# Recurrent output projection: six of eight channel tiles as high and low parts, one unit's low parts by GpSimd

## The chip, the cores and the metric

The kernel runs on one NeuronCore of a Trainium2 chip. Its engines are TensorE (PE in the rows; its weight loads are PEld), VectorE (DVE), ScalarE (ACT), GpSimd (POOL) and SyncE (SP), which here only issues DMAs. They run side by side and wait for each other through semaphores. The metric is the time of one execution on the device in microseconds, lower being better; the median of several runs counts.

## What is computed

A decoder trunk of two layers on 256 tokens of width 1024, all in float32. Layer 0 is latent attention and a dense SwiGLU; layer 1 is a gated linear recurrence and a mixture of 8 experts, two for each token. The change sits at the end of the recurrence:

```python
    _, hs = lax.associative_scan(combine, (a, b), axis=1)
    y = hs.astype(h.dtype) * gate_br
    return y @ w_out            # (256 x 1024) @ (1024 x 1024)
...
    # in the trunk
    h = h + mix
    hn = rmsnorm(h, norm_ffn[i])
    h = h + moe_swiglu(hn, moe_w_router[k], moe_w_gate[k], moe_w_up[k], moe_w_down[k])
    return rmsnorm(h, norm_final)
```

## The kernel before

Everything is written out by hand: each engine has its own program, in a fixed order, with explicit waits on semaphores. Tokens are two tiles of 128 (`t`), output columns two halves of 512 (`b`), and the 1024 channels over which the projection sums are eight tiles of 128 (`a`). Weights arrive in units of 128 x 2048 float32 (1 MB), each holding two channel tiles of `w_out`, in the six slots of `raw`. The four units of `w_out` are `L_OUT` to `L_OUT + 3`, in slots 3, 4, 5 and 0.

The kernel multiplies in float32 in two ways.

- **Directly** (line 1473): float32 operands, with the stationary side cut into four strips of 32 tokens that work beside each other in the array. Each matmul of the program leaves two records in the trace.
- **As high and low parts** (`product`, lines 424 to 426): both operands are split into a rounded high part (type float32r) and the remainder. Three products, high by high, high by low and low by high, are added up in PSUM, each 128 x 128 by 128 x 512. The high part is a copy by ScalarE (`copy`, line 791; `split_hi`, line 398), the low part a subtraction of two SBUF tensors by another engine (`split_lo`, line 404, and line 2114).

In the projection before, channel tiles 0 to 3 (units `L_OUT`, `L_OUT + 1`) go directly, tiles 4 to 7 as parts. The direct part starts when the first half of y (`states[:, 0:4]`) has been multiplied by the gate (`gated(0)`, line 2086, `y_ready` 1). While TensorE works on it, VectorE does the second half of the recurrence: one multiplication (line 2074), four scans along the tokens (line 2076), `gated(1)` (line 2086, `y_ready` 2), then `out_low(0)` (line 2114), the low part of y tiles 4 to 7 (line 2119) and `out_low(1)`. ScalarE makes the high parts: of unit `L_OUT + 2` into `w_hi[:, 2]`, of `L_OUT + 3` into the memory of `xTl_lru`, and of y tiles 4 to 7 into `y_split`. TensorE waits for `y_lo` and for each unit's `lo_done`.

What follows the projection is a chain of small steps: the residual sum (line 2132), transposes of it (line 1431), the router's logits (line 1443), the choice of experts, and the gathering of each expert's tokens (line 1506). Then the experts' matmuls (line 1500) run to the end of the program. GpSimd is not used in the projection. Behind its wait for `y_ready` 2 it issues three small loads (lines 725 to 727, among them `wr`, the router's weights, that line 2124 needs) and makes constants for the router (lines 728 to 744). SyncE loads the experts' units in a ring of 16 places (lines 609 to 616), some of which are the slots of `raw`: slot 5 and slot 0 come free by `lo_done`, slots 3 and 4 by `used`, all four in the projection.

Of the kernel before, what the change touches and what calls it, by code (L numbers as in the profile page):

```python
# [6 lines left out]
F32 = mybir.dt.float32  # L7
# [14 lines left out]
def trunk(nc, x, positions, norm_mix, norm_ffn, norm_final, mla_w_in, mla_q_norm, mla_kv_norm,  # L22
# [25 lines left out]
    with ExitStack() as ctx:  # L48
# [5 lines left out]


        raw = sb(ctx, "raw", [P, SLOTS, UNIT], F32)
        res = sb(ctx, "res", [P, TT, D], F32)
# [18 lines left out]
        with ExitStack() as split:  # L76
# [18 lines left out]
            with ExitStack() as s:  # L95
# [8 lines left out]
                with ExitStack() as s2:  # L104
                    a_sq = sb(s2, "a_sq", [P, KT // 2, T], F32)
                xch = sb(s, "xch", [P, 2, T], F32R)
                xcl = sb(s, "xcl", [P, 2, T], F32R)
# [101 lines left out]
        def lru_use(n):  # L209
            return n % SLOTS, LRU_BASE + n // SLOTS + 1  # L210
# [423 lines left out]
        def _(pool):  # L634
# [87 lines left out]
            pool.memset(x_br[:, :, 0:CONV - 1], 0.0).then_inc(pads, 1)  # L722
            token_roots()
            pool.wait_ge(y_ready, 2)
            pool.dma_start(gain_moe[:], norm_ffn[1].partition_broadcast(P)).then_inc(moe_in, 16)
# [63 lines left out]
        def _(act):  # L789
# [250 lines left out]
            gate_out(6, ACT.Gelu_apprx_tanh)  # L1040
            gate_out(7, ACT.Gelu_apprx_tanh)
            for n, place in ((0, 2), (1, 1)):
                s, c = lru_use(L_OUT + 2 + n)
                act.wait_ge(landed[s], c * 16)
                act.wait_ge(used[place], SPLIT_USES[place])
                copy(OUT_SPLIT[n][0], raw[:, s]).then_inc(hi_done[s], 1)
# [72 lines left out]
        def _(pe):  # L1119
# [345 lines left out]
            for t in range(TT):  # L1465
                for b in range(2):
                    for a in range(4):
                        s, n = lru_use(L_OUT + a // 2)
                        if t == 0 and b == 0 and a % 2 == 0:
                            pe.wait_ge(landed[s], n * 16)  # L1470
                        for rows_q in QUARTERS:
# [3 lines left out]
                                           stop=False, tile_position=(0, rows_q.start), skip_group_check=True)  # L1475
                        if (t, b) == (TT - 1, 1) and a % 2 == 1:
                            mm.then_inc(used[s], 1)

            pe.wait_ge(y_lo, 1)
            for t in range(TT):  # L1480
                for b in range(2):
# [225 lines left out]
        def _(dve):  # L1707
# [403 lines left out]
            def out_low(n):  # L2111
# [3 lines left out]
                                  ALU.subtract).then_inc(lo_done[s], 1)  # L2115

            out_low(0)
            dve.wait_ge(y_hi, 1)
            dve.tensor_tensor(y_split[:, 1], states[:, 4:KT], y_split[:, 0].bitcast(F32),
# [301 lines left out]
```

## Time and profile before

| | before |
|---|---|
| median of 3 runs | 1317.88 us (1317.78 to 1318.00) |
| the profiled execution, its own time | 1318.05 us |
| its span, first to last instruction | 1316.2 us |
| TensorE busy in the span | 1305.8 us (99%) |
| direct part of the projection (64 matmuls, 128 records) | 13.94 us |
| granted TensorE clock, mean | 1.000 |

The profile is of one execution. A row of the timeline gives the start in microseconds from the span's start, the duration, the engine, the line of the kernel, the operation, what it writes and reads, and how many instructions are merged in the row (x); in brackets stands how long the engine was idle before it and what ended that. The chain that ended last names what would have to be shorter for the program to end earlier.

### The profile page before, as it was taken

The numbers are of one execution on the slowest core, as the hardware profiler recorded it, in microseconds if no ns is written. First come the engines' busy times: TensorE is split into PE (matmuls) and PEld (weight loads), VectorE is DVE, ScalarE is ACT, GpSimd is POOL, SyncE is SP. The second block draws the span as 40 slices with busy tenths as digits, with TensorE's granted clock in tenths as the row PEclk, the third lists the DMA queues.
The fourth block names the chain that finished last, engine by engine and source line by source line (L and its number), as shares of the span: only waits on it lengthen the run. The fifth ranks groups of instructions, "written<-read, shape, count | busy, mean of one in ns | idle before, by whom it ended". The sixth has DMA issues, their size and how long they took to land.

```text
span 1316.2 us, 25501 instructions
## 1 busy us (share of the span) xinstructions
PE 1305.8 (99%) x10922; PEld 768.1 (58%) x10922; DVE 642.5 (49%) x1458; ACT 283.2 (22%) x424; POOL 86.9 (7%) x114
## 2 busy tenths in 40 slices
PE   9999999999999999999999999999999999999998
PEld 5778888888896544444444444444444444444444
DVE  5978666666776253432533523323353353342436
ACT  4874333333584100010010010001001001000102
POOL 2401111111001100000000000000000000000100
PEclk9999999999999999999999999999999999999999
DMA  7815555556467899999999999999999999999992
GB/s 278 306 61 179 193 191 191 191 191 203 153 250 307 314 412 403 420 410 413 420 420 405 418 420 408 419 412 408 408 420 409 407 420 419 406 400 420 419 415 90
DMA packets 124227, 441.92 MB, mean 336 GB/s; under 512 B 7294, under 2 KB 17600, under 8 KB 109536
## 3 DMA queue, kind: packets, MB, share of 16 engines
q1 hardware_dynamic: 119488, 424.57, 81.9%
q0 software_dynamic: 4624, 15.87, 3.3%
q8 instruction: 82, 1.34, 0.4%
q14 instruction: 17, 0.14, 0.0%
q10 hardware_dynamic: 16, 0.00, 0.0%
HBM read 430.84 MB, written 9.57 MB: 335 GB/s over the span
## 4 chain that ended last, share of the span: by engine, by line
PE 95%; DVE 2%; ACT 1%; DMA 1%; issue 0%; SPq 0%; DVEq 0%; POOL 0%
PE psum L1500 66%; PE psum L424 8%; PE psum L426 8%; PE psum L425 8%; DMA raw<-in_mla_w_uq 1%; PE psum L1473 1%; DVE w_lo L404 1%; PE psum L1506 0%; ACT res L880 0%; PE psum L1147 0%; PE psum L1348 0%; ACT gain_mla L791 0%; PE psum L440 0%; DVE res L1883 0%; ACT early L791 0%
## 5 line engine op out<-in xcount | busy, mean ns | idle before, releaser
L1500 PE MATMUL psum<-raw_more,hT 128*32 128x512 f32 x1656 | 535.7, 592 | 0.0
L1500 PE MATMUL psum<-raw,hT 128*32 128x512 f32 x1032 | 334.8, 592 | 0.0
L1500 PE MATMUL psum<-raw_more,xg_odd 128*32 128x512 f32 x1680 | 245.4, 592 | 0.0
L1500 PE MATMUL psum<-raw_more,xg 128*32 128x512 f32 x1704 | 241.8, 592 | 0.7 <-DVE xg L2212 0.7
L1500 PEld LDWEIGHTS psum<-raw_more,hT 128*32 128x32 f32 x1656 | 146.8, 109 | 122.6 <-issue 122.6
L2248 DVE STREAM_TRANSPOSE hT<-hid 32x128 f32<-32x128 f32 x672 | 204.9, 305 | 10.3
L2238 DVE SCALAR_TENSOR_TENSOR hid<-hid,psum 96x512 f32<-96x512 f32 x55 | 37.6, 684 | 303.3 <-PE psum L1500 302.5
L1092 ACT ACTIVATE hid<-psum 96x1024 f32<-96x1024 f32 (+1 forms) x32 | 29.2, 912 | 664.8 <-PE psum L1500 475.8
L1500 PE MATMUL psum<-raw,xg_odd 128*32 128x512 f32 x1008 | 147.7, 592 | 0.0
L1500 PE MATMUL psum<-raw,xg 128*32 128x512 f32 x984 | 144.2, 592 | 0.0
L1500 PEld LDWEIGHTS psum<-raw,hT 128*32 128x32 f32 x1032 | 91.1, 109 | 76.0 <-issue 75.8
L404 DVE TENSOR_TENSOR w_lo<-raw,w_hi 128x2048 fp32r<-128x2048 f32 (+1 forms) x53 | 119.6, 2276 | 30.6 <-ACT w_hi L398 30.5
L2225 DVE SCALAR_TENSOR_TENSOR hid<-hid,psum 96x1024 f32<-96x1024 f32 (+1 forms) x32 | 34.7, 1084 | 201.8 <-ACT hid L1092 201.8
L1500 PEld LDWEIGHTS psum<-raw_more,xg 128*32 128x32 f32 x1704 | 83.4, 110 | 83.5 <-issue 83.5
L1500 PEld LDWEIGHTS psum<-raw_more,xg_odd 128*32 128x32 f32 x1680 | 84.5, 110 | 77.9 <-issue 77.9
L398 ACT ACTIVATE w_hi<-raw 128x2048 fp32r<-128x2048 f32 (+1 forms) x60 | 111.4, 1889 | 19.4 <-PE psum L426 16.7
L424 PE MATMUL psum<-w_hi,xTh_ffn 128*128 128x512 f32 x224 | 87.3, 390 | 0.0
L426 PE MATMUL psum<-w_hi,xTl_ffn 128*128 128x512 f32 x224 | 87.2, 389 | 0.0
L425 PE MATMUL psum<-w_lo,xTh_ffn 128*128 128x512 f32 x224 | 87.2, 389 | 0.0
L1500 PEld LDWEIGHTS psum<-raw,xg_odd 128*32 128x32 f32 x1008 | 50.7, 110 | 46.8 <-issue 46.8
L1500 PEld LDWEIGHTS psum<-raw,xg 128*32 128x32 f32 x984 | 49.5, 110 | 47.9 <-issue 47.9
L791 ACT ACTIVATE y_main<-psum 32x512 f32<-32x512 f32 x48 | 28.4, 592 | 145.1 <-PE psum L1500 145.1
(318 smaller groups left out, 1343.7 us busy)
## 6 DMA issues: line engine op xcount, KB each, us to landing
raw_more<-in_moe_w_gate SPq DMA_DIRECT2D x71, 1024.0 KB, 16.2
raw_more<-in_moe_w_up SPq DMA_DIRECT2D x70, 1024.0 KB, 15.8
raw_more<-in_moe_w_down SPq DMA_DIRECT2D x69, 1024.0 KB, 16.8
raw<-in_moe_w_down SPq DMA_DIRECT2D x43, 1024.0 KB, 16.8
raw<-in_moe_w_up SPq DMA_DIRECT2D x42, 1024.0 KB, 16.2
raw<-in_moe_w_gate SPq DMA_DIRECT2D x41, 1024.0 KB, 17.2
raw<-in_ffn_w_gate SPq DMA_DIRECT2D x14, 1024.0 KB, 5.1
raw<-in_ffn_w_up SPq DMA_DIRECT2D x14, 1024.0 KB, 5.5
```

What stands on the lines that cost most here:

```text
L398: act.activation(w_hi[:, s, 0:width], raw[:, s, 0:width], ACT.Copy).then_inc(hi_done[s], 1)
L404: eng.tensor_tensor(w_lo[:, s, 0:width], raw[:, s, 0:width], w_hi[:, s, 0:width].bitcast(F32), ALU.subtract).then_inc(lo_done[s], 1)
L424: pe.matmul(out_ap, sh, mh, start=first, stop=False, **lone)
L425: pe.matmul(out_ap, sh, ml, start=False, stop=False, **lone)
L426: mm = pe.matmul(out_ap, sl, mh, start=False, stop=last, **lone)
L791: return act.activation(dst, src, ACT.Copy)
L1092: act.activation(hid[:, 0:WIDTH[m] * BANK].rearrange("p (a b) -> p a b", b=BANK), psum[SLOT_ROWS, 0:WIDTH[m]], ACT.Tanh, scale=0.5).then_i ...
L1473: mm = pe.matmul(psum[rows_q, 2 * t + b], states[:, a, c0:c0 + 32], unit(raw, s, D)[:, a % 2, b * BANK:(b + 1) * BANK], start=a == 0, stop ...
L1500: return pe.matmul(psum[rows_q, bank, cols], stationary, moving, start=start, stop=stop, tile_position=(0, rows_q.start), skip_group_check ...
L2225: dve.scalar_tensor_tensor(out=h, in0=h, scalar=1.0, in1=psum[SLOT_ROWS, 0:WIDTH[m]], op0=ALU.add, op1=ALU.mult).then_inc(m_mid, 1)
L2238: dve.scalar_tensor_tensor(out=hid[:, cols], in0=hid[:, cols], scalar=0.5, in1=psum[SLOT_ROWS, BANK_U[h]], op0=ALU.mult, op1=ALU.mult).the ...
L2248: ins = dve.transpose(hT[QUARTERS[to], H_BUF[j], :, QUARTERS[b]].rearrange("p (h r) s -> p h r s", r=2), hid[QUARTERS[b], h * BANK:(h + 1) ...
```

## The change

The second unit of `w_out`, `L_OUT + 1` with channel tiles 2 and 3, goes from the direct way to high and low parts. Direct are now tiles 0 and 1. Four instructions are new, one on ScalarE for the weights and one for y (`y_mid`, 128 x 512), one on VectorE for the low part of y, and one on GpSimd for the low part of the weights. GpSimd writes its result over the weights that it reads (`raw_lo` is the memory of `raw` under another type). The high part goes to `w_hi[:, 1]`. `y_mid` has the place of `a_sq`, which is no longer read by then. The new instructions stand ahead of those for tiles 4 to 7 on ScalarE and VectorE, and on GpSimd ahead of its wait for `y_ready` 2.

```diff
+        with ExitStack() as s:
+            raw_lo = sb(s, "raw_lo", [P, SLOTS, UNIT], F32R)
         raw = sb(ctx, "raw", [P, SLOTS, UNIT], F32)
...
+                with ExitStack() as s2:
+                    y_mid = sb(s2, "y_mid", [P, 2, KT // 4, T], F32R)
                 xch = sb(s, "xch", [P, 2, T], F32R)
...
             token_roots()
+            s, c = lru_use(L_OUT + 1)
+            pool.wait_ge(hi_done[s], c)
+            pool.tensor_tensor(raw_lo[:, s], raw[:, s], w_hi[:, 1].bitcast(F32),
+                               ALU.subtract).then_inc(lo_done[s], 1)
             pool.wait_ge(y_ready, 2)
...
             gate_out(7, ACT.Gelu_apprx_tanh)
+            s, c = lru_use(L_OUT + 1)
+            act.wait_ge(landed[s], c * 16)
+            act.wait_ge(used[1], SPLIT_USES[1])
+            copy(w_hi[:, 1], raw[:, s]).then_inc(hi_done[s], 1)
+            act.wait_ge(y_ready, 1)
+            copy(y_mid[:, 0], states[:, 2:4]).then_inc(y_hi, 1)
             for n, place in ((0, 2), (1, 1)):
...
-                    for a in range(4):
-                        s, n = lru_use(L_OUT + a // 2)
+                    for a in range(2):
+                        s, n = lru_use(L_OUT)
...
             pe.wait_ge(y_lo, 1)
+            for t in range(TT):
+                for b in range(2):
+                    s, n = lru_use(L_OUT + 1)
+                    tok, cols = slice(t * P, (t + 1) * P), slice(b * BANK, (b + 1) * BANK)
+                    hi, lo = (w.rearrange("p (a b) -> p a b", b=D) for w in (w_hi[:, 1], raw_lo[:, s]))
+                    product(pe, psum[:, 2 * t + b],
+                            [(y_mid[:, 0, a, tok], y_mid[:, 1, a, tok], hi[:, a, cols], lo[:, a, cols])
+                             for a in range(2)], start=False, stop=False,
+                            marks={1: used[s]} if (t, b) == (TT - 1, 1) else {},
+                            units={0: (s, n)} if (t, b) == (0, 0) else {})
+
+            pe.wait_ge(y_lo, 2)
...
+            dve.wait_ge(y_hi, 1)
+            dve.tensor_tensor(y_mid[:, 1], states[:, 2:4], y_mid[:, 0].bitcast(F32), ALU.subtract).then_inc(y_lo, 1)
             out_low(0)
-            dve.wait_ge(y_hi, 1)
+            dve.wait_ge(y_hi, 2)
```

VectorE around the end of the recurrence, before. `xn_lru` is the memory of `states`; the rows on line 2076 are the scans, 2086 is `gated(1)`:

```order
L2076 SCALAR_TENSOR_TENSOR xn_lru<-gain_lru,x_br 128x256 x3
L2086 TENSOR_TENSOR xn_lru<-xn_lru,gate_br 128x1024 [waits gelu_ready,state_ready]
L2074 TENSOR_TENSOR x_br<-x_br,xn_lru 128x4x256 [waits mult_ready]
L2076 SCALAR_TENSOR_TENSOR xn_lru<-gain_lru,x_br 128x256 [waits link_s]
L2076 SCALAR_TENSOR_TENSOR xn_lru<-gain_lru,x_br 128x256 x3
L2086 TENSOR_TENSOR xn_lru<-xn_lru,gate_br 128x1024 [waits gate_copied,state_ready]
L2114 TENSOR_TENSOR w_lo<-raw,w_hi 128x2048 [waits hi_done5]
L2119 TENSOR_TENSOR y_split<-xn_lru,y_split 128x1024 [waits y_hi]
L2114 TENSOR_TENSOR w_lo<-raw,xTl_lru 128x2048 [waits hi_done0]
L2124 TENSOR_TENSOR wr_gain<-wr,par 128x64 [waits moe_in]
```

And now, with lines shifted by the added ones (2102 scans, 2112 `gated(1)`, 2140 `out_low`):

```order
L2102 SCALAR_TENSOR_TENSOR xn_lru<-gain_lru,x_br 128x256 x3
L2112 TENSOR_TENSOR xn_lru<-xn_lru,gate_br 128x1024 [waits gelu_ready,state_ready]
L2100 TENSOR_TENSOR x_br<-x_br,xn_lru 128x4x256 [waits mult_ready]
L2102 SCALAR_TENSOR_TENSOR xn_lru<-gain_lru,x_br 128x256 [waits link_s]
L2102 SCALAR_TENSOR_TENSOR xn_lru<-gain_lru,x_br 128x256 x3
L2112 TENSOR_TENSOR xn_lru<-xn_lru,gate_br 128x1024 [waits gate_copied,state_ready]
L2144 TENSOR_TENSOR y_mid<-xn_lru,y_mid 128x512 [waits y_hi]
L2140 TENSOR_TENSOR w_lo<-raw,w_hi 128x2048 [waits hi_done5]
L2147 TENSOR_TENSOR y_split<-xn_lru,y_split 128x1024 [waits y_hi]
L2140 TENSOR_TENSOR w_lo<-raw,xTl_lru 128x2048 [waits hi_done0]
L2152 TENSOR_TENSOR wr_gain<-wr,par 128x64 [waits moe_in]
```

The low part of `y_mid` has come in between `gated(1)` and `out_low(0)`.

GpSimd at the same place, before (line 404 is its share of the dense layer's splits, long over):

```order
L643 DMA gain_lru<-in_norm_mix 128x1024 [waits xn_ready]
L722 MEMSET x_br 128x8x3
L667 TENSOR_TENSOR rstd<-rstd,half 128x1 [waits var_ready] x2
L725 DMA gain_moe<-in_norm_ffn 128x1024 [waits y_ready]
L726 DMA gain_out<-in_norm_final 128x1024
L727 DMA wr<-in_moe_w_router 128x8x8
L728 MEMSET ones 128x128
L729 MEMSET before 128x128
```

And now:

```order
L647 DMA gain_lru<-in_norm_mix 128x1024 [waits xn_ready]
L726 MEMSET x_br 128x8x3
L671 TENSOR_TENSOR rstd<-rstd,half 128x1 [waits var_ready] x2
L730 TENSOR_TENSOR raw_lo<-raw,w_hi 128x2048 [waits hi_done4]
L733 DMA gain_moe<-in_norm_ffn 128x1024 [waits y_ready]
L734 DMA gain_out<-in_norm_final 128x1024
L735 DMA wr<-in_moe_w_router 128x8x8
L736 MEMSET ones 128x128
L737 MEMSET before 128x128
```

The subtraction on the second unit stands in front of the loads, behind a wait for ScalarE's `hi_done4` alone.

## Rows read from the trace of the kernel before

**Rows 1.** The page: span, TensorE's time, its clock by slices, the chain by engine.
```profile
span 1316.2 us, 25501 instructions
PE 1305.8 (99%) x10922; PEld 768.1 (58%) x10922; DVE 642.5 (49%) x1458; ACT 283.2 (22%) x424; POOL 86.9 (7%) x114
...
PEclk9999999999999999999999999999999999999999
...
PE 95%; DVE 2%; ACT 1%; DMA 1%; issue 0%; SPq 0%; DVEq 0%; POOL 0%
```

**Rows 2.** TensorE's waits, whole span: who waited for whom, total, times, longest.
```profile
PE psum L1132 <- DVE zeros L1784: 1.1, 1, 1.1
```

**Rows 3.** Timeline of TensorE in the projection: direct part, then parts.
```profile
402.72 13.94 PE L1473 MATMUL psum<-raw,xn_lru 128*32 128x512 f32 x128 [0.73 <-issue]
...
409.59 0.16 PEld L1473 LDWEIGHTS psum<-raw,xn_lru 128*32 128x32 f32 x4 [0.27 <-issue]
...
416.59 0.50 PE L424 MATMUL psum<-w_hi,y_split 128*128 128x512 f32 x1
...
416.93 0.39 PE L425 MATMUL psum<-w_lo,y_split 128*128 128x512 f32 x1
...
422.17 0.39 PE L424 MATMUL psum<-w_hi,y_split 128*128 128x512 f32 x1
```

**Rows 4.** The same timeline, rows of ScalarE, VectorE and GpSimd.
```profile
402.31 1.91 ACT L791 ACTIVATE w_hi<-raw 128x2048 fp32r<-128x2048 f32 x1
...
403.79 2.44 DVE L2076 TENSOR_TENSOR_SCAN xn_lru<-gain_lru,x_br 128x256 f32<-128x256 f32 x4
...
406.26 1.23 DVE L2086 TENSOR_TENSOR xn_lru<-xn_lru,gate_br 128x1024 f32<-128x1024 f32 x1
...
407.41 2.29 DVE L2114 TENSOR_TENSOR w_lo<-raw,w_hi 128x2048 fp32r<-128x2048 f32 x1
...
407.52 1.06 ACT L791 ACTIVATE y_split<-xn_lru 128x1024 fp32r<-128x1024 f32 x1 [1.50 <-DVE xn_lru L2086]
407.79 0.58 POOL L725 DMA_DIRECT2D gain_moe<-in_norm_ffn  x1 [61.20 <-DVE xn_lru L2086]
...
409.61 1.22 DVE L2119 TENSOR_TENSOR y_split<-xn_lru,y_split 128x1024 fp32r<-128x1024 f32 x1
...
410.75 2.38 DVE L2114 TENSOR_TENSOR w_lo<-raw,xTl_lru 128x2048 fp32r<-128x2048 f32 x1
```

**Rows 5.** Line 404 in the dense layer: count, minimum/median/maximum ns of one.
```profile
L404 POOL TENSOR_TENSOR w_lo<-raw,w_hi x7: 4618/4618/4623, 122.3 to 318.8; 128x2048 fp32r<-128x2048 f32 x7
```

**Rows 6.** Timeline of VectorE in the dense layer, beside GpSimd's 122.31 to 126.93.
```profile
122.19 0.68 DVE L1962 SCALAR_TENSOR_TENSOR hid_f<-hid_f,psum 128x512 f32<-128x512 f32 x1
...
123.74 5.05 DVE L1984 STREAM_TRANSPOSE xn_ffn<-hid_f 32x128 f32<-32x128 f32 x16
...
129.62 0.68 DVE L1976 TENSOR_TENSOR hTl_f<-xn_ffn,hTh_f 128x512 fp32r<-128x512 f32 x1
```

**Rows 7.** Timeline of VectorE in the attention's projections.
```profile
38.30 2.31 DVE L404 TENSOR_TENSOR w_lo<-raw,w_hi 128x2048 fp32r<-128x2048 f32 x1
...
40.53 2.83 DVE L404 TENSOR_TENSOR w_lo<-raw,w_hi 128x2048 fp32r<-128x2048 f32 x1
```

**Rows 8.** Timeline of GpSimd in the same stretch.
```profile
38.54 2.66 POOL L691 TENSOR_TENSOR k<-q,trig 128x256 f32<-128x256 f32 x1
...
45.81 0.81 POOL L696 TENSOR_TENSOR k<-q,trig 128x256 f32<-128x256 f32 x1
```

**Rows 9.** Timeline of VectorE behind the projection.
```profile
414.68 0.23 DVE L2124 TENSOR_TENSOR wr_gain<-wr,par 128x64 f32<-128x64 f32 x1 [1.56 <-DMA wr<-in_moe_w_router]
...
419.65 0.69 DVE L2132 TENSOR_TENSOR res<-res,psum 128x512 f32<-128x512 f32 x1 [4.74 <-PE psum L426]
```

**Rows 10.** Timeline, start of the experts' matmuls.
```profile
438.52 20.81 PE L1500 MATMUL psum<-raw_more,xg 128*32 128x512 f32 x192 [0.74 <-DVE xg L2212]
```

**Rows 11.** DMA of experts' stage, 438 to 1316 us: issues by line, KB, median us to landing.
```profile
raw<-in_moe_w_gate SPq DMA_DIRECT2D x37, 1024.0 KB, 17.4
```

More of the change, by code:

```diff
@@ L1466, in _ @@
                 for b in range(2):
-                    for a in range(4):
-                        s, n = lru_use(L_OUT + a // 2)
-                        if t == 0 and b == 0 and a % 2 == 0:
+                    for a in range(2):
+                        s, n = lru_use(L_OUT)
+                        if t == 0 and b == 0 and a == 0:
                             pe.wait_ge(landed[s], n * 16)
@@ L1475, in _ @@
                                            stop=False, tile_position=(0, rows_q.start), skip_group_check=True)
-                        if (t, b) == (TT - 1, 1) and a % 2 == 1:
+                        if (t, b) == (TT - 1, 1) and a == 1:
                             mm.then_inc(used[s], 1)
             pe.wait_ge(y_lo, 1)
+            for t in range(TT):
[9 more added lines that the diff above has]
+            pe.wait_ge(y_lo, 2)
             for t in range(TT):
```

## The prediction

> **What bounds the kernel now.** I read the page first: TensorE is busy for 1305.8 of 1316.2 us, its clock digit is 9 in all 40 slices, and the chain that ended last lies on it for 95% [rows 1]. Then its waits: the longest of the whole execution is 1.1 us [rows 2]. So the projection costs what TensorE spends on it, as long as the operands come in time, and every microsecond saved or lost there moves the end. The timeline shows the two ways at work. The direct part starts at 402.72 and takes 13.94 us, and the parts follow at 416.59 [rows 3]. During the direct part VectorE is never idle: scans from 403.79, `gated(1)` from 406.26, `out_low(0)` from 407.41 [rows 4]. So the direct part is also what hides the end of the recurrence, and the change halves that cover.
>
> **TensorE, removed.** The direct part is 32 equal groups of four records, and tiles 2 and 3 are half of them. It fills the time from 402.72 to the next part's start at 416.59, less 0.11 for the change of kind (below): 13.76 us, half of it 6.88. So it would end at 409.60; the weight loads still run at their even pace there [rows 3].
>
> **TensorE, added.** Four outputs by two tiles by three products are 24 products of 128 x 128 by 128 x 512. The next stage has the same ones: the second starts at 416.93 and the 25th at 422.17, 23 steps or 0.228 us each [rows 3]. 24 of them are 5.47 us. The first one after the direct way takes 0.34 (416.59 to 416.93), 0.11 more than the others, once before as now. Work on TensorE: 5.47 - 6.88 = -1.41 us, if it never waits.
>
> **When the operands of the new part are there.** TensorE is ready for it at 409.60 + 0.11 = 409.71. It needs the low part of the weights (GpSimd) and of y (VectorE).
>
> ScalarE: the copy of the unit takes the place of the one at 402.31, 1.91 us, to 404.22. Its data landed long before, since the direct part read them from 402.7 on. The copy of `y_mid` is 128 x 512, at most the 1.06 us of the 128 x 1024 one [rows 4], so it ends before 405.3. The other two weight copies end by about 409, still ahead of VectorE's use.
>
> GpSimd: idle for 61.2 us at this point [rows 4], so it starts when ScalarE is done, about 404.30. One 128 x 2048 subtraction takes 4.62 us there, seven times alike [rows 5]: ready at 408.92. Taken alone that is 0.8 us early.
>
> VectorE: `gated(1)` ends at 407.49 and the next may start at 407.41. The low part of `y_mid` costs 0.68, as the 128 x 512 one of the dense layer [rows 6]: ready at 408.09. Taken alone that is 1.6 us early.
>
> **The two together.** GpSimd's 4.62 us were measured beside VectorE instructions that read PSUM or one SBUF tensor: a product with `psum`, then transposes [rows 6]. In the projection VectorE runs only instructions with two SBUF inputs. Another stretch of the trace has such pairs. There GpSimd's 128 x 256 product took 2.66 us where the same form took 0.81 later [rows 8]: it was started at 38.54, in the middle of VectorE's subtraction from 38.30 to 40.61, and ended at 41.20, 0.59 after it. VectorE's next subtraction started at 40.53 and took 2.83 instead of 2.31 [rows 7], 0.52 longer. So one waits for the other to end, in both directions, and VectorE loses nearly all of GpSimd's time.
>
> The Trainium skill says the same ("SBUF — State Buffer", section "Who interferes with whom"): a VectorE instruction with two SBUF inputs contends with a GpSimd instruction that reads SBUF, and whichever comes first keeps the shared ports for the whole instruction. Here it speaks against the change: by it the sum is a loss, without it the sum is the gain of TensorE's work. The trace's pair of rows agrees with it.
>
> The new subtraction is eight times as long as the 128 x 256 product. VectorE's loss of 0.52 us times eight is 4.2 us; GpSimd's own 4.62, less some 0.2 of its start outside the ports, is 4.4. I take 4.3. The bounds are 0 (nothing shared) and 4.62. Where in VectorE's row the block falls does not matter: GpSimd asks at 404.3, during the first or second scan, and everything from there to the low part of `y_mid` is behind it. So that low part is ready at 408.09 + 4.3 = 412.39, and TensorE sees it some 0.05 later (407.49 to 407.52 from VectorE to ScalarE [rows 4]), at 412.44.
>
> **Sum.** TensorE waits 412.44 - 409.71 = 2.73 us. The sum is -1.41 + 2.73 = +1.32 us. The new part then runs from 412.44 to about 418.0.
>
> **What is late next.** On VectorE `out_low(0)` (2.29) follows to 414.6, then the low part of `y_split` (1.22; ScalarE's copy for it waits for `gated(1)`, now 411.8, and ends at 412.9) to 415.8, then `out_low(1)` (2.38) to 418.1 [rows 4]. TensorE needs the first two at 418.0 and the third six products later, at 419.4: no wait, with 1.3 us to spare. On GpSimd the three loads and the router's constants stand behind `y_ready` 2 and move by 4.3 us: `wr` lets line 2124 start at 419.0 instead of 414.68, and the residual sum behind it on VectorE is due at 419.65 + 1.32 = 421.0 [rows 9]. Slots 5, 0, 3 and 4 of the ring are released up to 5 us later, the last at about 418.2; landing takes 17.4 us where DMA is fullest [rows 11], to 435.6, before the experts' matmuls start at 438.52 [rows 10]. All three cost nothing, but `wr` has only 2 us of cover.
>
> **The rivals.**
>
> A, the forecast: GpSimd blocks VectorE from the scans on. +1.32 us, with 4.2 to 4.62 for the block +1.2 to +1.7.
>
> B, scans do not share with GpSimd, only the two-input products do. No row has a scan beside GpSimd. Then GpSimd runs 404.30 to 408.92 beside the scans, `gated(1)` starts at about 408.85 instead of 406.26, and the low part of `y_mid` comes 2.6 late, at 410.7. The wait is 410.75 - 409.71 = 1.04: -0.37 us.
>
> C, nothing is shared, or GpSimd's start slips behind VectorE's row without harm. Then both operands are early: -1.41 us. For it speaks only that GpSimd's long subtraction never met a second reader before; against it the rows at 38.54 and 40.53.
>
> D, slower than can be overlooked: TensorE's clock. TensorE would stand still for 2.7 us, over twice the 1.1 us of its longest wait so far, in which the clock never left 2.4 GHz (digit 9 throughout, rows 1). If it falls to 1.2 GHz in that gap, each of the 24 products costs another 0.23 us for as long as that lasts: all of them +5.5, half of them +2.7. Half gives +1.32 + 2.7 = +4.0 us, 1321.9. It decides from 6 slow products on (+1.3, in sum over 0.2%). Against it: the gap is short, and the engine is dense on both sides. The Trainium skill names this ("TensorE: Matmul & The Clock Gate", section "What's actually happening"): an idle TensorE is given 1.2 GHz instead of 2.4. No row here shows an idle stretch long enough.
>
> E, `wr` or the experts' units come late. This adds to A only what exceeds 2 us of cover; I give it with D's chance.
>
> **The numbers.** A 0.63, B 0.14, C 0.11, D and E 0.12. The profiled execution took 1318.05, the median of the three runs was 1317.88, 0.17 less. The likeliest is 1317.88 + 1.32 = 1319.2 us. C gives 1316.5, B 1317.5, A 1319.1 to 1319.6. The range must leave out no more than 0.2; without D and E it holds 0.88, and with some room for A's latencies it is 1316.3 to 1320.4. What a measurement can tell from no change is 0.2%, 2.6 us. A, B and C all lie within it: same 0.86. C plus something unseen would have to gain 2.6 us: faster 0.02. Slower 0.12, from D and E.
>
> **What would show it.** In the changed kernel's timeline: 64 records of the direct part in about 6.9 us; GpSimd's subtraction from 404.3, about 4.6 us long; one scan or `gated(1)` over 4 us longer than the rest, and `gated(1)` ending at about 411.8; TensorE idle for 2.7 us ahead of its first product with `y_mid`, released by VectorE; 24 products in 5.5 us; experts' matmuls starting at 439.9. If `gated(1)` still ends at 407.5, it is C; if the scans keep their pace and `gated(1)` is late by 2.6, it is B; products of over 0.4 us apiece behind the gap, with a clock under 1.00, are D. The forecast is wrong above all if GpSimd gives way to VectorE piece by piece, which no row of before can tell for so long an instruction.

## The result, and the profile after

The changed kernel takes 1321.12 us (median of 15 runs, 1319.41 to 1322.78) against 1318.02 us of the kernel before (15 runs on the same chips, 1317.18 to 1321.86). The ratio is 1.0024 with a 95% interval of 1.0017 to 1.003: slower by about 3 us, just over the 0.2% that the prediction took for the smallest difference that can be told. The forecast was 1319.2 us, the range ended at 1320.4. The same kernel in ten more runs gave 1320.96 (1319.01 to 1321.95), ratio 1.0025 [1.0016, 1.0035].

From the page of the changed kernel, the lines that answer to [rows 1], and behind them TensorE's waits as in [rows 2]:

```profile
span 1319.4 us, 25427 instructions
PE 1306.6 (99%) x10882; PEld 771.9 (59%) x10882; DVE 645.6 (49%) x1459; ACT 285.5 (22%) x426; POOL 92.1 (7%) x115
...
PE 93%; DVE 3%; ACT 2%; DMA 1%; issue 0%; SPq 0%; DVEq 0%; POOL 0%
```
```profile
PE psum L428 <- DVE y_mid L2144: 2.7, 1, 2.7
PE psum L1146 <- DVE zeros L1810: 1.1, 1, 1.1
```

The list of waits has one new row at its head, 2.7 us for the low part of `y_mid`. The chain lost two points on TensorE and has one more on VectorE and one on ScalarE. But TensorE's busy time did not fall, as 1.41 us less work would have it; it rose from 1305.8 to 1306.6. A wait does not add to the busy time, so something else is there beside it. The timeline of the projection shows the rest (columns: start, us, engine, line, operation, count, idle time before and what ended it). It answers to [rows 3] and [rows 4]:

```profile
402.48 7.07 PE L1487 MATMUL psum<-raw,xn_lru 128*32 128x512 f32 x64 [0.73 <-issue]
403.55 6.82 DVE L2102 TENSOR_TENSOR_SCAN xn_lru<-gain_lru,x_br 128x256 f32<-128x256 f32 x4
...
404.05 4.61 POOL L730 TENSOR_TENSOR raw_lo<-raw,w_hi 128x2048 fp32r<-128x2048 f32 x1 [57.70 <-ACT w_hi L799]
...
410.41 1.23 DVE L2112 TENSOR_TENSOR xn_lru<-xn_lru,gate_br 128x1024 f32<-128x1024 f32 x1
411.55 0.68 DVE L2144 TENSOR_TENSOR y_mid<-xn_lru,y_mid 128x512 fp32r<-128x512 f32 x1
...
412.29 0.50 PE L428 MATMUL psum<-w_hi,y_mid 128*128 128x512 f32 x1 [2.73 <-DVE y_mid L2144]
...
412.63 0.40 PE L429 MATMUL psum<-raw_lo,y_mid 128*128 128x512 f32 x1
412.86 0.59 PE L430 MATMUL psum<-w_hi,y_mid 128*128 128x512 f32 x1
...
413.25 0.63 PE L428 MATMUL psum<-w_hi,y_mid 128*128 128x512 f32 x1
...
413.68 0.63 PE L429 MATMUL psum<-raw_lo,y_mid 128*128 128x512 f32 x1
...
416.24 0.43 PE L429 MATMUL psum<-raw_lo,y_mid 128*128 128x512 f32 x1
...
416.51 0.40 PE L430 MATMUL psum<-w_hi,y_mid 128*128 128x512 f32 x1
```

One of the four scans holds nearly all of GpSimd's time. Asked for alone:

```profile
404.16 5.05 DVE L2102 TENSOR_TENSOR_SCAN xn_lru<-gain_lru,x_br 128x256 f32<-128x256 f32 x1
```

Three things are to be seen. The second scan takes 5.05 us, where four together took 2.44 [rows 4]; it starts at 404.16, when GpSimd's subtraction (404.05 to 408.66) has just begun, and ends after it. TensorE then stands still for 2.73 us. And the products behind the gap first start 0.23 us apart (412.63 to 412.86), then 0.43 (413.25 to 413.68), and from 416.51 on 0.23 again. By stretches (columns: length, busy time and count of TensorE, of its weight loads, of VectorE, ScalarE and GpSimd, granted TensorE clock as a share of full speed, share of DMA, GB/s):

```profile
409.60:412.20 2.60, 0.00 (x0) 0.00 (x0) 2.56 (x5) 0.53 (x1) 0.27 (x1) 1.00 0.00 0
412.30:416.20 3.90, 3.90 (x10) 3.07 (x11) 3.90 (x3) 0.43 (x1) 3.82 (x10) 0.58 0.72 222
416.30:419.50 3.20, 3.20 (x15) 2.61 (x14) 1.79 (x2) 0.00 (x0) 1.72 (x1) 1.00 0.91 257
```

The granted clock is still 1.00 in the gap itself. It falls to 1.2 GHz some 0.6 us after TensorE has begun again (it is 1.00 from 412.30 to 412.80 and 0.50 from 413.20 on), and comes back some 3.4 us later: a mean of 0.58 over the 3.9 us of the second row. From 412.86 to 416.24 there are 8 products in 3.38 us, 0.42 each. That is rival D, on top of the forecast A. The clock digit of the page reads 9 in all 40 slices as before: a slice is 33 us, and this dip is a tenth of one. The windows show it, the page doesn't.

What lies behind:

```profile
418.74 0.22 DVE L2152 TENSOR_TENSOR wr_gain<-wr,par 128x64 f32<-128x64 f32 x1 [0.87 <-DMA wr<-in_moe_w_router]
...
422.46 0.69 DVE L2160 TENSOR_TENSOR res<-res,psum 128x512 f32<-128x512 f32 x1 [3.49 <-PE psum L430]
...
441.26 5.31 PE L1526 MATMUL psum<-raw_more,xg 128*32 128x512 f32 x45 [0.75 <-DVE xg L2240]
```

From the residual sum to the experts' matmuls it is 18.80 us, before it was 18.87 [rows 9, 10]: nothing is lost or given back behind the projection. So the distance from the start of the direct part to the start of the experts' matmuls measures the change without the scatter of whole executions (about 1 us either way), though in one profiled execution of each kernel. It was 35.80 us before (402.72 to 438.52 [rows 3, 10]) and is 38.78 now: +2.98. Below it is called **the stretch**.

### The profile page after: what moved, and what is told of

The parts are those of the page before. It is cut to its first block, busy times and chain, and to the rows that moved or that the text cites. A ratio compares the mean times of both kernels' runs of the same rounds, so it can differ in the third digit from the quotient of the medians.

```text
span 1319.4 us, 25427 instructions
## 1 busy us (share of the span) xinstructions
PE 1306.6 (99%) x10882; PEld 771.9 (59%) x10882; DVE 645.6 (49%) x1459; ACT 285.5 (22%) x426; POOL 92.1 (7%) x115
## 3 DMA queue, kind: packets, MB, share of 16 engines
q8 instruction: 82, 1.34, 0.4%
## 4 chain that ended last, share of the span: by engine, by line
PE 93%; DVE 3%; ACT 2%; DMA 1%; issue 0%; SPq 0%; DVEq 0%; POOL 0%
PE psum L1526 66%; PE psum L428 8%; PE psum L430 8%; PE psum L429 8%; DMA raw<-in_mla_w_uq 1%; DVE w_lo L408 1%; DVE xn_lru L2102 1%; ACT res L888 0%; PE psum L1532 0%; ACT gain_mla L799 0%; PE psum L1161 0%; ACT gain_lru L1003 0%; ACT early L799 0%; PE psum L1362 0%; PE psum L444 0%
```

## Experiments

Two theories. **Theory 1**: the loss is A plus D, which means GpSimd's read of SBUF blocks VectorE for its whole length, TensorE waits 2.7 us for it, and the pause lowers its clock for a while. **Rival**: the loss comes from the new way itself (the slow products from something in the new part, such as its operands or the DMA traffic that starts at 413; the wait from GpSimd's result coming late, not from blocking).

### The same kernel again

No edit.

> The changed kernel once more, beside the next one on the same chip. From the runs so far: the waiting part of the loss, +1.3 to +1.5 us over the kernel before, is in every execution, and the fall of the clock behind the gap is not always of the same size, so single times scatter more than those of the kernel before, from about +1.3 to about +4 us, with the median near +3. If the profiled execution shows another share of slow products than the eight of the first one, its time should differ by 0.2 us for each product more or less. Rival: the loss of the clock is fixed, every execution has eight slow products and the scatter is that of the kernel before (about 1.5 us).

Measured: 1320.96 us as given above. The profiled execution was one without the dip:

```profile
412.53 0.50 PE L428 MATMUL psum<-w_hi,y_mid 128*128 128x512 f32 x1 [2.74 <-DVE y_mid L2144]
...
440.06 3.21 PE L1526 MATMUL psum<-raw_more,xg 128*32 128x512 f32 x28 [0.75 <-DVE xg L2240]
```
```profile
412.60:416.60 4.00, 4.00 (x17) 3.23 (x18) 4.00 (x3) 0.37 (x1) 3.85 (x11) 1.00 0.76 198
```

The wait is the same, 2.74 us, but 17 products start in the 4 us behind it and the clock stays at 1.00. The direct part starts at 402.72 here, so the stretch is 37.34 us: +1.54 over before. The two traces of one kernel differ by 38.78 - 37.34 = 1.44 us, which is what the dip costs. Operands and DMA traffic are alike in both (0.76 and 0.72 of the DMA, even at the same place), so the rival's slow products are out: the same operands and the same traffic go with either pace. Over all 25 executions of this kernel the mean granted clock was 1.000 in 6 (mean 1319.85 us) and 0.999 or 0.998 in 19 (mean 1321.38 us), 1.5 us apart. A dip of 3.4 us at half speed takes 1.7 us of 1318 from the mean clock, 0.0013: the right size for 0.999. The mean has three digits, so by the same sum a dip of under 1.3 us still reads 1.000, and the 0.998 of two of the ten repeated executions, the two slowest, would be 4 us or more at 1.2 GHz. No trace of those two exists, so the eight slow products are the count of one trace and not of every dip. All 20 runs of the kernel before on that chip show 1.000.

### Work in the gap

Behind the direct part and ahead of the wait for `y_mid`, 36 products of zeros in bfloat16 go to a PSUM bank that nobody reads (`keep_busy` is a function that the kernel has for such products); all else is the changed kernel.

```
+            pe.wait_ge(gate_copied, KT)
+            keep_busy(36, 7)
             pe.wait_ge(y_lo, 1)
```

> The changed kernel with 36 small products of zeros put on TensorE in the gap ahead of the first product with y_mid (they write to a bank that nobody reads and change no result). They fill about 2.5 of the 2.73 us that TensorE stood still. Theory 1, the gap costs twice, once as waiting (2.73 us) and once more because the clock falls to 1.2 GHz behind it (eight products at 0.43 instead of 0.23 us, +1.6): with the filler the clock stays at 1.000, all 24 products take 0.23 us, the experts' matmuls start at about 439.9, and the time is 1.3 to 1.5 us over the kernel before. Rival, the slow products come from something that the stage itself does (GpSimd's loads, the memory of the new operands): they stay at 0.43 us and the time stays about 3.1 us over the kernel before.

```profile
410.53 2.19 PE L1146 MATMUL psum<-zeros 128*128 128x128 bf16 x36
...
413.34 0.50 PE L428 MATMUL psum<-w_hi,y_mid 128*128 128x512 f32 x1 [0.62 <-DVE y_mid L2146]
```

Measured: 1319.26 us (11 runs, 1318.59 to 1320.65) against 1318.09 of before, ratio 1.001 [1.0001, 1.0019]. The block is untouched (the same 6.82 us of scans), the products follow at 0.23 us, the clock is 1.000 in all 11 executions, and the stretch is 37.24 us, +1.44. So it is the pause that lowers the clock, and without the dip the change costs what A says. Work that computes nothing takes the change's loss from 3.0 us to 1.2.

### Half of that work

The same with 18 products, so that a shorter pause is left.

```
-            keep_busy(36, 7)
+            keep_busy(18, 7)
```

> The changed kernel with 18 small products of zeros ahead of the wait, half as many as in the run that filled the gap: about 1.1 us of work and then 1.6 us in which TensorE stands still. Shows which gap the clock stands. If only a gap near the full 2.7 us makes it fall, all products stay at 0.23 us and the time is +1.3 to +1.5 us over the kernel before; if 1.6 us is enough, the slow products are back and the time is near +3.

```profile
409.23 1.18 PE L1146 MATMUL psum<-zeros 128*128 128x128 bf16 x18
...
412.02 0.50 PE L428 MATMUL psum<-w_hi,y_mid 128*128 128x512 f32 x1 [1.61 <-DVE y_mid L2146]
```

Measured: 1319.45 us (11 runs, 1318.56 to 1321.19) against 1317.4, ratio 1.0014 [1.0005, 1.0023]; stretch 37.35 us, +1.55; clock 1.000 in all 11. A pause of 1.61 us shows no dip and costs only itself. The medians are 2.1 us apart, more than the stretch has; the interval, 0.7 to 3.0 us, holds both.

### GpSimd's subtraction twice

A second subtraction of the same size ahead of the first one, into a buffer that nothing reads yet. VectorE waits for GpSimd's second result ahead of `out_low(1)`, which writes this buffer.

```
+            link(pool.tensor_tensor(w_lo[:, 1], raw[:, s], w_hi[:, 1].bitcast(F32), ALU.subtract))
             pool.tensor_tensor(raw_lo[:, s], raw[:, s], w_hi[:, 1].bitcast(F32),
                                ALU.subtract).then_inc(lo_done[s], 1)
...
+            dve.wait_ge(lo_done[lru_use(L_OUT + 1)[0]], lru_use(L_OUT + 1)[1])
             out_low(1)
```

> The changed kernel with GpSimd's subtraction done twice, one behind the other (the first result goes to memory that is overwritten later). Theory 1, GpSimd's reading blocks VectorE for its whole length: VectorE gets in one scan between the two and then loses another 4.3 us or so, gated(1) ends at about 416, TensorE waits about 7 us instead of 2.73, and the waiting part of the loss grows by 4.3 to 4.6 us. The slow products behind the gap: if the clock's fall costs a fixed stretch, again about eight products at 0.43 us (+1.6), in sum +7.3 to +7.8 us over the kernel before; if it grows with the gap, all 24 are slow (+4.9) and the sum is about +11. Rival to theory 1, that VectorE was held up only once by something at the start: the wait stays near 2.7 us and the time near +3.

```profile
402.74 11.07 DVE L2103 TENSOR_TENSOR_SCAN xn_lru<-gain_lru,x_br 128x256 f32<-128x256 f32 x4
...
403.23 4.61 POOL L730 TENSOR_TENSOR w_lo<-raw,w_hi 128x2048 fp32r<-128x2048 f32 x1 [57.70 <-ACT w_hi L800]
...
407.92 4.76 POOL L731 TENSOR_TENSOR raw_lo<-raw,w_hi 128x2048 fp32r<-128x2048 f32 x1
...
415.73 0.79 PE L428 MATMUL psum<-w_hi,y_mid 128*128 128x512 f32 x1 [6.98 <-DVE y_mid L2145]
```
```profile
412.00:413.00 1.00, 0.00 (x0) 0.00 (x0) 1.00 (x1) 0.00 (x0) 0.68 (x1) 0.84 0.00 0
413.00:415.70 2.70, 0.00 (x0) 0.00 (x0) 2.67 (x5) 0.59 (x1) 0.33 (x1) 0.50 0.00 0
415.70:419.60 3.90, 3.87 (x9) 3.10 (x10) 3.90 (x3) 0.46 (x1) 3.83 (x10) 0.51 0.67 210
```

Measured: 1325.11 us (4 runs, 1324.25 to 1325.28) against 1317.4, ratio 1.0056 [1.0041, 1.0072]. The scans take 11.07 us instead of 6.82, 4.25 more for the second subtraction: the whole length counts, once per instruction. The wait is 6.98 us, the stretch +7.36. The mean clock is below 1.000 in all four executions. In the trace it falls within the pause: TensorE stops at about 408.75, the clock is 1.00 until 412.00, 0.84 over the next microsecond and 0.50 from 413.00 to 415.70, while TensorE does nothing. So it is low from the first product on (0.79 us for it, where 0.50 is usual), and it comes back at about 419.4. That is 6.7 us at 1.2 GHz, twice as long as in the first trace, which agrees with a mean clock of 0.997; but only 3.6 us of it, 8 slow products, fall on work. In these two traces the dip thus costs about the same, though this pause was two and a half times as long.

### GpSimd's subtraction in quarters

The same 128 x 2048 elements as four instructions of 128 x 512.

```
+            for n in range(4):
+                part = slice(n * BANK, (n + 1) * BANK)
+                ins = pool.tensor_tensor(raw_lo[:, s, part], raw[:, s, part], w_hi[:, 1, part].bitcast(F32),
+                                         ALU.subtract)
+            ins.then_inc(lo_done[s], 1)
```

> The changed kernel with GpSimd's subtraction cut into four of 128 x 512. If the two engines take turns instruction by instruction, three scans and gated(1) each lose one quarter of about 1.1 us, the sum for VectorE is the same 4.3 to 4.5 us, gated(1) ends at about 411.7, TensorE waits about 2.7 us as in the changed kernel, and GpSimd ends later than 408.7, at about 410.6. If the holder keeps the ports as long as it has more to do, the picture is that of the changed kernel with one scan of 5 us. If pieces slip between VectorE's instructions for free, the wait shrinks below 2 us.

```profile
403.56 5.61 DVE L2105 TENSOR_TENSOR_SCAN xn_lru<-gain_lru,x_br 128x256 f32<-128x256 f32 x4
...
404.07 6.17 POOL L732 TENSOR_TENSOR raw_lo<-raw,w_hi 128x512 fp32r<-128x512 f32 x4 [57.70 <-ACT w_hi L802]
...
405.32 1.67 POOL L732 TENSOR_TENSOR raw_lo<-raw,w_hi 128x512 fp32r<-128x512 f32 x1
...
405.83 1.71 DVE L2105 TENSOR_TENSOR_SCAN xn_lru<-gain_lru,x_br 128x256 f32<-128x256 f32 x1
...
409.21 2.11 DVE L2115 TENSOR_TENSOR xn_lru<-xn_lru,gate_br 128x1024 f32<-128x1024 f32 x1
...
411.98 0.50 PE L428 MATMUL psum<-w_hi,y_mid 128*128 128x512 f32 x1 [2.41 <-DVE y_mid L2147]
```

Measured: 1319.62 us (10 runs, 1318.6 to 1321.49) against 1317.4, ratio 1.0017 [1.0008, 1.0027]; stretch of a profiled execution without the dip 37.01 us, +1.21. The rows at 405.32 and 405.83 are one quarter and one scan asked for alone. The engines take turns: a quarter takes 1.67 us and three of the scans 1.7 each instead of 0.6. GpSimd's four pieces need 6.17 us, where the one piece needed 4.61, the scans 5.61 instead of 6.82, and the last quarter makes `gated(1)` 2.11 instead of 1.23. All of it is still ahead of `y_mid`, so the wait is 2.41 us; I had expected 2.7, nearly the same as in one piece. Smaller pieces share the loss out, they don't remove it. By chance this gives another length of pause: at 2.41 us the mean clock is below 1.000 in 5 of 10 executions, and those 5 take 1320.6 us in the mean, the other 5 take 1319.05.

### The subtraction alone, with the kernel before

The kernel before, with one added subtraction by GpSimd at the same place, for which VectorE waits ahead of `out_low(0)`; its result is not used.

```
+            s, c = lru_use(L_OUT + 2)
+            pool.wait_ge(hi_done[s], c)
+            pool.wait_ge(used[1], SPLIT_USES[1])
+            pool.tensor_tensor(w_hi[:, 1], raw[:, s], w_hi[:, 2].bitcast(F32), ALU.subtract).then_inc(pool_link, 1)
...
+            dve.wait_ge(pool_link, tried[0])
             out_low(0)
```

> The kernel before with one instruction of the change alone: a subtraction by GpSimd of 128 x 2048 from 404.2 on (unit L_OUT + 2 less its high part, into memory that nobody reads), and out_low(0) waiting for it. All four channel tiles stay direct. Theory 1: VectorE's scans and gated(1) are held up by 4.3 us as in the changed kernel, gated(1) ends at about 411.8, but TensorE is in its direct part until 416.5 and needs nothing before, so out_low(0) at 414 and the low part of y at 415.3 still come in time: no wait, the time is that of the kernel before within 0.3 us. So the same block is free there and costs 2.73 us in the changed kernel only because the cover was halved. Rival, the block also costs elsewhere (the router's weights, the loads): the time is up by 1 us or more.

```profile
403.26 6.80 DVE L2083 TENSOR_TENSOR_SCAN xn_lru<-gain_lru,x_br 128x256 f32<-128x256 f32 x4
...
403.77 4.59 POOL L728 TENSOR_TENSOR w_hi<-raw,w_hi 128x2048 fp32r<-128x2048 f32 x1 [57.70 <-ACT w_hi L798]
...
437.90 9.65 PE L1507 MATMUL psum<-raw_more,xg 128*32 128x512 f32 x88 [0.71 <-DVE xg L2220]
```

Measured: 1317.8 us (10 runs, 1317.28 to 1320.04) against 1317.4, ratio 1.0003 [0.9994, 1.0012]; stretch 35.71 us, -0.09. VectorE loses the same 4.4 us (6.80 against 2.44 for the scans), and the end doesn't move: a direct part of 13.94 us covers it, one of 7.07 doesn't. I had put `out_low(0)` at 414; it started at 411.24, which only leaves more cover. So the block by itself costs nothing.

### GpSimd only writes

In place of the subtraction, two fills of the same 128 x 2048. The low part of the unit is left out of the sum by this.

```
-            pool.tensor_tensor(raw_lo[:, s], raw[:, s], w_hi[:, 1].bitcast(F32),
-                               ALU.subtract).then_inc(lo_done[s], 1)
+            link(pool.memset(raw_lo[:, s].bitcast(F32), 0.0))
+            pool.memset(raw_lo[:, s].bitcast(F32), 0.0).then_inc(lo_done[s], 1)
```

> The changed kernel with two fills with zeros by GpSimd in the place of its subtraction, so the low part of the added unit's weights is left out of the sum. Both theories agree that GpSimd is busy from 404.1; the fills take about 1.9 us each and read nothing. If it is GpSimd's reading of SBUF that stops VectorE's two-input instructions, the four scans take 2.4 us as before, TensorE never waits, and the time is about -1.4 us against the kernel before. If any GpSimd instruction on SBUF stops VectorE, gated(1) ends about 3.7 us late, as long as the fills are, and the time is about +0.7 us or more.

```profile
404.16 2.44 DVE L2102 TENSOR_TENSOR_SCAN xn_lru<-gain_lru,x_br 128x256 f32<-128x256 f32 x4
...
404.63 1.81 POOL L730 MEMSET raw_lo<- 128x2048 f32 x1 [57.68 <-ACT w_hi L799]
...
406.50 1.80 POOL L731 MEMSET raw_lo<- 128x2048 f32 x1
```

Measured: 1317.15 us (10 runs, 1315.96 to 1317.86) against 1318.09, ratio 0.9992 [0.9982, 1.0001]; stretch 34.44 us, -1.36. GpSimd is busy from 404.63 to 408.30, beside the last three scans, `gated(1)` and the low part of `y_mid`, and they keep their 2.44, 1.22 and 0.68 us. TensorE does not wait. It is GpSimd's reading that blocks, and with it gone, what remains is the saved work. The halved direct part without the block costs nothing either: neither half of the change does by itself.

### GpSimd reads one tensor

The subtraction is replaced by a copy of `w_hi`. The unit's low part is left out of the sum by this, and its high part stands in its place.

```
-            pool.tensor_tensor(raw_lo[:, s], raw[:, s], w_hi[:, 1].bitcast(F32),
-                               ALU.subtract).then_inc(lo_done[s], 1)
+            pool.tensor_copy(raw_lo[:, s], w_hi[:, 1]).then_inc(lo_done[s], 1)
```

> The changed kernel with a copy of the high part by GpSimd in the place of its subtraction: one SBUF input instead of two, the same write. The low part is wrong by that, so the high part is counted twice in one product and the result is not that of the reference. From 128 x 512 in 0.75 us elsewhere I take 2.8 us for it. If one reading stream of GpSimd is enough to stop VectorE's two-input instructions, VectorE loses about 2.6 us, gated(1) ends at about 410 and TensorE waits about 1 us. If it takes two streams, the scans keep their pace and TensorE never waits.

```profile
402.73 4.08 DVE L2101 TENSOR_TENSOR_SCAN xn_lru<-gain_lru,x_br 128x256 f32<-128x256 f32 x4
...
403.21 1.90 POOL L730 CAST raw_lo<-w_hi 128x2048 fp32r<-128x2048 f32 x1 [57.69 <-ACT w_hi L798]
```

Measured in one profiled execution: 1316.02 us; stretch 34.51 us, -1.29. I had sized the copy at 2.8 us, it took 1.90, so that it is too short for a wait. The scans lose 4.08 - 2.44 = 1.64 us of its 1.90: one stream of reads blocks as two do, for nearly as long as the instruction lasts.

### VectorE does the subtraction itself, last

GpSimd's part is left out; VectorE makes the low part of the unit behind that of `y_mid`.

```
             dve.tensor_tensor(y_mid[:, 1], states[:, 2:4], y_mid[:, 0].bitcast(F32), ALU.subtract).then_inc(y_lo, 1)
+            s, c = lru_use(L_OUT + 1)
+            dve.wait_ge(hi_done[s], c)
+            dve.tensor_tensor(raw_lo[:, s], raw[:, s], w_hi[:, 1].bitcast(F32), ALU.subtract).then_inc(lo_done[s], 1)
```

> The changed kernel with the low part of the added unit by VectorE, behind the low part of y_mid, and nothing by GpSimd. If GpSimd's hold on the shared reading is what delayed VectorE by 4.3 us, the scans and gated(1) are back at their pace, gated(1) ends at about 407.3, the unit's low part at 410.2; TensorE waits about 0.8 us instead of 2.7, the clock stays at 2.4 GHz, and the time is -1.4 + 0.8 = about -0.6 us against the kernel before. Rival, VectorE was late for another reason (ScalarE's copies): gated(1) stays at about 411.6 and the time stays at or above +1.3 us.

```profile
407.29 2.28 DVE L2143 TENSOR_TENSOR raw_lo<-raw,w_hi 128x2048 fp32r<-128x2048 f32 x1
...
409.72 0.47 PE L428 MATMUL psum<-w_hi,y_mid 128*128 128x512 f32 x1 [0.64 <-DVE raw_lo L2143]
```

Measured: 1316.9 us (11 runs, 1316.27 to 1317.76) against 1318.09, ratio 0.9991 [0.9982, 1.0]; stretch 35.09 us, -0.71. GpSimd's 4.61 us were to take work off VectorE. On VectorE it takes 2.28 us, half of what the help costs it.

### VectorE does it first

Both low parts, of `y_mid` and of the unit, stand between the scans and `gated(1)`: they need neither the gate nor the second half of the states.

```
             recurrence(1)
+            dve.wait_ge(y_hi, 1)
+            dve.tensor_tensor(y_mid[:, 1], states[:, 2:4], y_mid[:, 0].bitcast(F32), ALU.subtract).then_inc(y_lo, 1)
+            s, c = lru_use(L_OUT + 1)
+            dve.wait_ge(hi_done[s], c)
+            dve.tensor_tensor(raw_lo[:, s], raw[:, s], w_hi[:, 1].bitcast(F32), ALU.subtract).then_inc(lo_done[s], 1)
             gated(1)
```

> A version that should beat both: the low parts of y_mid and of the added unit by VectorE, directly behind the scans and ahead of gated(1), nothing by GpSimd. VectorE: scans to 406.0, y_mid's low part to 406.6, the unit's to 408.8, before TensorE is ready at 409.5; gated(1) to 410.0, the rest to 415.7, needed at 416.5. TensorE never waits, so the whole gain of its work, -1.4 us against the kernel before, with a clock of 1.000. If the order costs more than I think (the last low part late, or the router's weights, that come 2.8 us later), TensorE waits at the third product group of the next part or the residual sum is late, and the gain is under 1 us.

```profile
404.98 0.67 DVE L2132 TENSOR_TENSOR y_mid<-xn_lru,y_mid 128x512 fp32r<-128x512 f32 x1
...
405.57 2.28 DVE L2135 TENSOR_TENSOR raw_lo<-raw,w_hi 128x2048 fp32r<-128x2048 f32 x1
...
407.77 1.22 DVE L2108 TENSOR_TENSOR xn_lru<-xn_lru,gate_br 128x1024 f32<-128x1024 f32 x1
...
408.56 0.50 PE L428 MATMUL psum<-w_hi,y_mid 128*128 128x512 f32 x1
...
417.24 0.69 DVE L2159 TENSOR_TENSOR res<-res,psum 128x512 f32<-128x512 f32 x1 [0.48 <-PE psum L430]
```

Measured: 1316.62 us (11 runs, 1315.26 to 1319.6) against 1318.09, ratio 0.999 [0.9981, 0.9999]; stretch 34.54 us, -1.26. TensorE goes from the direct part straight to the products.

### The same again, beside the changed kernel

> The version with both low parts by VectorE ahead of gated(1), once more beside the changed kernel on the same chip: -1.4 us against the kernel before, about -4.4 against the changed kernel, and no execution with a clock under 1.000 in the projection.

Measured on one chip: 1316.83 us (11 runs, 1315.4 to 1318.03), the kernel before 1317.98, the changed kernel 1320.96. Ratio to before 0.9992 [0.9983, 1.0001], stretch 34.46 us, -1.34. This is the best version found: 4.1 us faster than the changed kernel, with the same products on TensorE; 4.4 was expected. Against the kernel before it is 1.2 to 1.5 us faster by medians and 1.3 by the stretch. One of the two intervals just includes no change, so by whole executions alone the gain is likely rather than settled.

All of them in one table, stretch and median as differences to the kernel before (median: of the runs on the same chip):

| kernel | wait of TensorE | stretch | median | clock below 1.000 |
|---|---|---|---|---|
| changed | 2.73 | +2.98 | +3.1 | 12 of 15 |
| changed again | 2.74 | +1.54 | +3.0 | 7 of 10 |
| work in the gap | 0.62 | +1.44 | +1.2 | 0 of 11 |
| half of it | 1.61 | +1.55 | +2.1 | 0 of 11 |
| subtraction twice | 6.98 | +7.36 | +7.7 | 4 of 4 |
| in quarters | 2.41 | +1.21 | +2.2 | 5 of 10 |
| subtraction alone | 0 | -0.09 | +0.4 | 0 of 10 |
| GpSimd writes only | 0 | -1.36 | -0.9 | 0 of 10 |
| GpSimd reads one | 0 | -1.29 | (one run) | 0 of 1 |
| VectorE, last | 0.64 | -0.71 | -1.2 | 0 of 11 |
| VectorE, first | 0 | -1.26 | -1.5 | 1 of 11 |
| VectorE, first, again | 0 | -1.34 | -1.2 | 0 of 11 |

One execution of the kernel with VectorE first shows 0.999 without a pause in the projection, at 1319.6 us, its slowest; no trace of that execution exists. A mean below 1.000 alone is thus not quite proof of a dip at this place, but the kernel before shows it in none of its 80 executions beside the experiments.

## Why the prediction was wrong, point by point

**TensorE's work: right.** -1.41 us was forecast. With all waits gone the stretch is shorter by 1.26 to 1.36 us. In the changed kernel the direct part and the turn to the next kind took 7.07 us rather than 6.99. The 24 products took 5.65 us rather than 5.47 (412.53 to 418.29 in the repeated trace, less the first one's 0.11), since they start 0.236 us apart and not 0.228, the pace I had read from the next stage.

**The block: right, in cause and size.** The scans went from 2.44 to 6.82, 4.38 us; 4.3 was forecast, from two workings. One was GpSimd's duration less 0.2, and it holds in the runs: 4.61 less 0.23 here, 4.59 less 0.23 with the kernel before, 1.90 less 0.26 for the copy. The other, eight times the 0.52 us of a row, came near by luck: GpSimd's time does not grow eightfold with the size, since 0.81 us for 128 x 256 [rows 8] would be 6.5 and not 4.6. Forecast: `gated(1)` ends at 411.8, TensorE waits 2.73. Measured: 411.64 with everything 0.24 earlier, and 2.73 us, to the digit because TensorE and `y_mid` were both ready 0.08 us later than forecast. The rule of the Trainium skill ("SBUF — State Buffer", section "Who interferes with whom") holds here in the parts that a run touched: a GpSimd instruction that reads holds a VectorE instruction with two inputs, one that only writes doesn't, and GpSimd's instruction, once begun, keeps VectorE out to its end (the 5.05 us scan ends 0.55 us behind it). The rivals B and C fell with this: the scan is blocked too (B), and GpSimd neither waits nor gives way piece by piece (C).

**What is late next: right.** `wr_gain` at 418.74 (forecast 419.0), no further wait, 18.80 us from the residual sum to the experts. E didn't happen.

**Case A's sum: +1.32 forecast, +1.44 to +1.55 measured** in the traces without a dip (the changed kernel and the two with products of zeros). The difference is mostly the 0.08 and the 0.18 us above.

**The step that failed: the clock.** It was rival D, put at 0.12 together with E, priced at half of the 24 products and left out of the likeliest sum and of the range. The mechanism was named and the place was right; its chance and its size were not. By the mean clock it happens in 19 of 25 executions, so it is the usual case rather than the exception. In the trace it slows 8 products, not 12, and it costs 1.44 us (1.5 between the means of executions), not 2.7. With that the sum is +1.54 + 1.44 = +2.98, 1320.9 us; 1321.12 and 1320.96 were measured. The reason for the small chance was that "the gap is short, and the engine is dense on both sides". No row of the kernel before had a pause between 1.1 us and 2.7, so nothing in it spoke for that sentence. The 1.1 us pause lay ahead of TensorE's first instruction; between products the longest was 0.9. And a digit 9 for a slice of 33 us would not show a dip of 3.4. With a forecast pause three times the longest one between products, the rows gave no ground for putting D far below an even chance, and the upper end of the range should have held A and D together.

With a pause of 2.73 us the trace shows the clock at 1.00 in the pause and 0.58 in the 3.9 us behind it; the repeated trace shows no fall. With a pause of 6.98 us it was 1.00 for the first 3.2 us and 0.50 over the last 2.7. The Trainium skill ("TensorE: Matmul & The Clock Gate", section "What's actually happening") says that an idle TensorE is given 1.2 GHz. The trace of the long pause agrees, with 0.50 of 2.4 GHz. That the clock can also fall behind a shorter pause, when TensorE is at work again, and that the outcome varies at one and the same pause, is what the runs add.

What stays open: what decides between a dip and none at one and the same pause. The same kernel gives both, on one chip, and no trace shows a difference ahead of the gap. Pauses between 1.61 and 2.41 us were not tried. The two kernels with products of zeros were not measured beside the changed kernel. What ties their 0 of 22 to the shorter pause is that the changed kernel showed the dip in both of its own batches (12 of 15 and 7 of 10), and that the quarters, on one chip with the 1.61 us pause, showed it in 5 of 10. Nor was VectorE's own order tried with GpSimd's subtraction moved to a place where VectorE reads PSUM only.

## What to carry to other kernels

Work that reads SBUF, given to GpSimd beside VectorE, was free in the projection only where what waited for VectorE had cover for GpSimd's whole duration. It also depends on what VectorE runs: in the dense layer of the kernel before, beside the same subtraction, VectorE's transposes of one tensor [rows 6] took 0.30 us each, the same as those behind its end. Here the help cost VectorE 4.4 us, while doing the work itself costs 2.28. When a change takes cover away from one engine and adds work on another, look at both together: each half alone cost nothing here, and together they made a wait. And price a pause of TensorE of 2.4 us or more with the slow products behind it: 8 of them here, 1.4 us on top of the pause's 2.7; here some work without a use in the gap was cheaper than that, and doing the subtraction on VectorE in a better order was cheaper still.

## What the runs showed of the hardware

- **A scan is held up by GpSimd's reads, as other VectorE instructions with two SBUF inputs are.** A 128 x 256 scan took 5.05 us instead of 0.6 beside GpSimd's subtraction of 4.61 us.
- **The engines take turns by instruction.** Four quarters: scans 5.61, `gated(1)` 2.11, GpSimd 6.17 us for what took it 4.61 in one piece.
- **One stream of GpSimd's reads is enough** (1.64 us lost of a 1.90 us copy); none, and nothing is lost (two fills of 1.8 us, scans 2.44).
- **A pause of TensorE can lower its clock, and longer ones did it more often**: 0 of 11 at 1.61 us (and 0 of 11 at 0.62), 5 of 10 at 2.41, 19 of 25 at 2.73, 4 of 4 at 6.98. These counts tell 1.61 us from 2.41 and more; between 2.41, 2.73 and 6.98 they are too few. In one trace of each, the slow part was 8 products long both at 2.73 and at 6.98 us.
- **The clock can fall in the pause or behind it**: 0.50 over the last 2.7 us of the 6.98 us pause, 1.00 throughout the 2.73 us one and 0.50 from some 0.6 us behind it.
- GpSimd takes 4.6 us for a float32 subtraction of 128 x 2048, VectorE 2.28; GpSimd's copy of that size takes 1.90, its fill 1.81.
